# A hybrid decoder step on one core: the first projection from unnormed x, with the gates' and weights' first steps reordered

## The reference

```
h    = rmsnorm(x, norm1_w)              # x * rsqrt(mean(x^2) + 1e-6) * norm1_w, per token
proj = h @ w_in                         # columns: z, xBC, dt, u, q, k, v, and three gates
y_a  = SSD mixer(z, xBC, dt)            # causal conv, chunked scan, gated norm
y_b  = S5 mixer(u)                      # 32 groups of 16 channels, complex diagonal scan, GELU, GLU
y_c  = sliding-window attention(q, k, v)
mixed = sum over branches of sigmoid(gate) * (y @ w_branch)
x = x + mixed @ w_out
x = x + swiglu(rmsnorm(x, norm2_w)); y = rmsnorm(x, norm_f)
```

## Time and profile before

| | us |
|---|---|
| median of 3 runs | 1686.39 (1685.58 to 1688.41) |
| span of the profiled execution, first to last instruction | 1684.5 |
| TensorE busy | 1654.0 (98%) |
| VectorE, ScalarE, GpSimd busy | 966.9, 556.0, 791.2 |
| first product of u | 17.30 |
| first product of gate 0 | 69.16 |
| first product of gate 3 | 114.97 |

### The profile page before, as it was taken

The page is one execution under the profiler, slowest core; times in us unless marked ns, Lnnn a source line. Parts: engine busy times, 40 slices in busy tenths (PEclk is TensorE's granted clock), DMA queues, the critical chain, the costliest instruction groups (busy, mean ns, idle before and its releaser), DMA issues. The chain is left out here.

```text
span 1684.5 us, 30884 instructions
## 1 busy us (share of the span) xinstructions
PE 1654.0 (98%) x12241; PEld 1604.7 (95%) x12241; DVE 966.9 (57%) x1642; ACT 556.0 (33%) x1240; POOL 791.2 (47%) x756
## 2 busy tenths in 40 slices
PE   7999999999999999999999999999999999999997
PEld 7999999999999998888899999999999999999997
DVE  6859811406634554778873289666665565744346
ACT  5332121342213332543411154443443333322233
POOL 5483122322221111141322325877777777787774
PEclk9999999999999999999999999999999999999998
DMA  5364363232233234434365431543433344966443
GB/s 209 84 127 133 104 203 98 89 92 91 87 93 103 89 130 134 161 115 140 126 218 191 152 126 42 180 162 145 151 141 141 141 167 165 367 224 267 162 187 103
DMA packets 95805, 245.85 MB, mean 146 GB/s; under 512 B 14369, under 2 KB 42273, under 8 KB 95417
## 3 DMA queue, kind: packets, MB, share of 16 engines
q1 hardware_dynamic: 73824, 174.48, 30.5%
q0 software_dynamic: 10256, 33.59, 6.7%
q10 hardware_dynamic: 11592, 35.96, 6.3%
HBM read 177.11 MB, written 66.65 MB: 145 GB/s over the span
## 5 line engine op out<-in xcount | busy, mean ns | idle before, releaser
L1642 PE MATMUL ps<-HL,WH 128*128 128x384 f32 (+1 forms) x1536 | 507.7, 331 | 4.4 <-DVE HL L691 1.8
L1643 PE MATMUL ps<-HH,WL 128*128 128x384 f32 (+1 forms) x1536 | 497.4, 324 | 0.0
L1644 PE MATMUL ps<-HH,WH 128*128 128x384 f32 (+1 forms) x1536 | 496.3, 323 | 0.0
L1642 PEld LDWEIGHTS ps<-HL,WH 128*128 128x128 f32 x1536 | 289.4, 188 | 15.6 <-issue 9.3
L1643 PEld LDWEIGHTS ps<-HH,WL 128*128 128x128 f32 x1536 | 289.7, 189 | 0.3
L1644 PEld LDWEIGHTS ps<-HH,WH 128*128 128x128 f32 x1536 | 289.6, 189 | 0.0
L1285 POOL TENSOR_TENSOR WL<-WRAW,WH 128x1024 fp32r<-128x1024 f32 x59 | 145.0, 2457 | 243.3 <-DMA WH<-in_w 243.3
L1282 POOL DMA_DIRECT2D WH<-in_w x59 | 34.6, 586 | 354.4 <-PE ps L1644 352.9
L2932 DVE TENSOR_TENSOR X<-X,ps 128x528 f32<-128x528 f32 (+2 forms) x170 | 107.9, 656 | 155.5 <-PE ps L2238 104.6
L2327 ACT ACTIVATE GT<-ps 128x384 f32<-128x384 f32 (+1 forms) x72 | 33.4, 465 | 215.5 <-PE ps L1644 183.5
L2932 DVE TENSOR_TENSOR RB<-RB,ps 128x528 f32<-128x528 f32 x60 | 42.1, 701 | 103.4 <-ACT RB L2847 85.9
(11 more groups left out here) (467 smaller groups left out, 4266.2 us busy)
## 6 DMA issues: line engine op xcount, KB each, us to landing
WRAW<-in_w SPq DMA_DIRECT2D x75, 512.0 KB, 3.4
ffn_scratch<-STG SPq DMA_DIRECT2D x70, 528.0 KB, 3.6
WH<-in_w POOLq DMA_DIRECT2D x62, 512.0 KB, 4.6
SOP<-ffn_scratch SPq DMA_DIRECT2D x36, 528.0 KB, 7.9
gate_scratch<-GT ACTq DMA_DIRECT2D x24, 528.0 KB, 3.2
PX<-gate_scratch ACTq DMA_DIRECT2D x22, 528.0 KB, 4.2
HL<-ffn_scratch SPq DMA_DIRECT2D x22, 528.0 KB, 10.4
RAWB<-in_w SPq DMA_DIRECT2D x10, 1024.0 KB, 6.2
```

What stands on the lines that cost most here:

```text
L1642: nc.tensor.matmul(out, wh, rl, start=start, stop=False)
L1643: nc.tensor.matmul(out, wl, rh, start=False, stop=False)
L1644: return nc.tensor.matmul(out, wh, rh, start=False, stop=stop)
```

## The change

The first chunk of u is made from x times the norm weight, without the division by the root mean square. The products start as soon as x and the weights are split; the norm of that chunk is worked out later, and the tiles of u are multiplied by it on VectorE as they leave PSUM (`evict_first_u_dve`). The first chunk's h itself is split last (`SPLIT_ORDER` 1, 2, 0), as only the gates need it. The squares of a chunk are added in wider operations. Weights 0 and 1 are loaded as four halves from ScalarE's queue; SP's queue goes x, units 2 and 3, the second chunk of x, the bucket tables, the third chunk. The low parts of units 0 to 4 move from GpSimd to VectorE; GpSimd only counts them, and does the S5 constants earlier. TensorE starts with 92 products of a zeroed 128 x 128 tile. Of the gates, gate 0 takes its first chunk last, gate 1 follows at once, and taps and transposes of W come a gate later.

The core of the diff:

```diff
+    ROOT_ORDER = (1, 0, 2)
+    SPLIT_ORDER = (1, 2, 0)
+    FIRST_BY_ACT, SECOND_BY_ACT, SECOND_ADDS, THIRD_ADDS = 6, 6, 5, 5
...
+    def x_plain_high_act(k):
+        nc.scalar.wait_ge(s_x[k], 16)
...
+        nc.scalar.mul(HH[:, k, 0:384], X0[:, k, 0:384], prm("norm1", k, 1)).then_inc(xp_hi, 1)
+    def x_plain_low_dve(k):
+        dve.wait_ge(xp_hi, k + 1)
+        dve.scalar_tensor_tensor(HL[:, k, 0:384], X0[:, k, 0:384], prm("norm1", k, 1), HH[:, k, 0:384].bitcast(F32),
+                                 ALU.mult, ALU.subtract).then_inc(xp_lo, 1)
...
+    def x_second_sum_dve():
+        dve, pairs = nc.vector, GT[:, 0:768].rearrange("p (k c) -> p k c", c=384)
+        dve.wait_ge(s_xc[1], 128)
+        dve.tensor_tensor(pairs, X0[:, 6:8, 384:768], X0[:, 6:8, 384:768], ALU.mult).then_inc(pq_used, 1)
+        dve.wait_ge(pq_done, FIRST_BY_ACT + 4)
+        dve.tensor_tensor(SQ[:, 0:2], SQ[:, 0:2], SQ[:, 2:4], ALU.add).then_inc(pq_used, 1)
+        dve.wait_ge(pq_used, 2)
+        dve.tensor_tensor(SQ[:, 0:2], SQ[:, 0:2], pairs, ALU.add).then_inc(pq_used, 1)
+        dve.wait_ge(pq_done, FIRST_BY_ACT + SECOND_BY_ACT)
+        dve.wait_ge(pq_used, 3)
+        dve.tensor_tensor(SQ[:, 0:2], SQ[:, 0:2], HF0[:], ALU.add).then_inc(pq_used, 1)
+        dve.wait_ge(pq_used, 4)
+        dve.tensor_tensor(ACC[:, 384:768], SQ[:, 0], SQ[:, 1], ALU.add).then_inc(pq_used, 1)
...
+    def x_root_copy_act():
+        nc.scalar.wait_ge(pn_rs, 2)
+        nc.scalar.copy(GT[:, 0:384], x_spread_at(0)[:, 0:384]).then_inc(r0_ok, 1)
+    def evict_first_u_dve(j):
+        dve.wait_ge(r0_ok, 1)
+        dve.wait_ge(acc_done[0], j + 1)
+        dve.tensor_tensor(as_steps(UF[:, j, :], 0, 3), as_blocks(u_bank(j, 0), 3), as_blocks(GT[:, 0:384], 3),
+                          ALU.mult).then_inc(acc_free[0], 1)
...
         x_chunk(0)
+        first_weights(2)
+        first_weights(3)
+        x_chunk(1)
         sp.dma_start(HOT[:], io["hot"]).then_inc(s_hot, 16)
         sp.dma_start(RTAB[:], io["rtab"]).then_inc(s_hot, 16)
-        first_weights(0)
-        first_weights(1)
-        first_weights(2)
-        x_chunk(1, range(4))
-        x_chunk(1, range(4, KD))
-        first_weights(3)
...
+        nc.gpsimd.memset(IDB[:], 0.0).then_inc(consts_ok, 1)
...
+        def first_lows_counted():
+            pool.wait_ge(half_ok, 6)
+            pool.sem_inc(split_ok, 4)
+        def gate_low_counted():
+            pool.wait_ge(half_ok, 7)
+            pool.sem_inc(split_ok, 1)
...
         s5_angles()
-        split_halves()
-        u = 2
+        first_lows_counted()
+        s5_powers()
+        s5_rows()
+        s5_squarings(0)
+        gate_low_counted()
+        u = 5
...
+        pe.wait_ge(consts_ok, 2)
+        for _ in range(92):
+            nc.tensor.matmul(bank[4][:, 0:P], IDB[:], IDB[:], start=True, stop=True)
         pe.wait_ge(s_par, 16)
-        x_first_sums_pe()
-        bias_by_distance(0)
-        bias_by_distance(1)
-        x_spread_pe(0)
         u_pair(0, 0)
-        pe.wait_ge(bias_ev, 2)
-        u_pair(2, 0, {1: lambda: x_sums_pe(1), 3: lambda: x_spread_pe(1)})
-        u_pair(0, 1)
-        u_pair(2, 1, {1: lambda: x_sums_pe(2), 3: lambda: x_spread_pe(2)})
+        u_pair(2, 0, {1: lambda: bias_by_distance(0), 2: lambda: bias_by_distance(1), 3: lambda: x_sums_pe(1),
+                      5: lambda: x_spread_pe(1)})
+        u_pair(0, 1, {1: lambda: x_sums_pe(0), 5: lambda: x_spread_pe(0)})
+        u_pair(2, 1, {2: lambda: x_sums_pe(2), 4: lambda: x_spread_pe(2)})
         u_pair(0, 2)
         u_pair(2, 2)
...
-        gate(0, [0, 1])
+        gate(0, [1, 2])
+        gate(0, [0], lambda n, k: pe.wait_ge(h_lo, 2 * KD + k + 1))
+        gate(1, [0, 1])
         taps(0)
-        gate(0, [2])
         taps(1)
-        gate(1, [0])
+        gate(1, [2])
         taps(2)
-        gate(1, [1])
         taps(3)
-        gate(1, [2])
+        gate(2, [0])
         stt_rows(0)
-        for n in range(3):
-            gate(2, [n])
-            stt_rows(n + 1)
+        stt_rows(1)
+        gate(2, [1])
+        stt_rows(2)
+        gate(2, [2])
+        stt_rows(3)
...
+        for half in range(2):
+            c = slice(512 * half, 512 * half + 512)
+            for u in range(2):
+                act.dma_start(WRAW[:, u, c], io["w"][u][:, c]).then_inc(s_half0 if half == 0 else s_raw[u], 16)
...
+        for k in range(4, KD):
+            x_split_act(k, k + 1)
+            x_squares_act(2, [k])
+            if k == 6:
+                x_root_copy_act()
         evict_u(0, 1)
         evict_u(1, 1)
-        x_split_act(16, 24)
+        x_root_act(2)
+        x_split_act(8, 12)
         evict_u(2, 1)
+        x_split_act(12, 14)
         evict_u(3, 1)
+        x_split_act(14, 18)
+        evict_u(0, 2)
+        x_split_act(18, 19)
+        high_weights(4)
+        x_split_act(19, 20)
+        evict_u(1, 2)
+        x_split_act(20, 22)
+        high_weights(5)
+        x_split_act(22, 24)
...
+        x_plain_low_dve(0)
+        low_half_weights(0)
+        for k in range(1, 4):
+            x_plain_low_dve(k)
+        low_half_weights(1)
+        for k in range(4, KD):
+            x_plain_low_dve(k)
+        for u in (2, 3):
+            dve.wait_ge(first_high, u + 3)
+            tt(high_low(u)[1], WXR[:, u - 2, :], high_low(u)[0].bitcast(F32), ALU.subtract).then_inc(half_ok, 1)
         dve.wait_ge(den_ok, 1)
         nc.vector.reciprocal(SF("den"), SF("den")).then_inc(den_inv, 1)
+        x_first_rest_dve()
+        x_second_sum_dve()
+        x_first_add_dve(0)
+        x_recip_dve(1)
+        x_first_add_dve(1)
+        x_first_add_dve(2)
+        x_split_dve(0, 4)
+        x_recip_dve(0)
+        x_split_dve(4, 8)
+        x_third_sum_dve()
+        for j in range(3):
+            evict_first_u_dve(j)
         x_recip_dve(2)
+        evict_first_u_dve(3)
+        x_split_dve(8, 20)
+        dve.wait_ge(first_high, 7)
+        tt(high_low(4)[1], WRAW[:, 0, :], high_low(4)[0].bitcast(F32), ALU.subtract).then_inc(half_ok, 1)
+        x_split_dve(20, 24)
```

More of the change, by code:

```diff
@@ new lines, in x_first_squares_act, with x_first_rest_dve, x_first_add_dve @@
+    def x_first_squares_act(ks):
+        for k in ks:
+            nc.scalar.activation(SQ0[:, k, :], X0[:, k, 0:384], ACT.Square).then_inc(pq_done, 1)
+    def x_first_rest_dve():
+        dve, rest = nc.vector, slice(FIRST_BY_ACT, KD)
+        dve.tensor_tensor(SQ0[:, rest], X0[:, rest, 0:384], X0[:, rest, 0:384], ALU.mult).then_inc(x0_add, 1)
+    def x_first_add_dve(i):
+        dve = nc.vector
+        if i == 0:
+            dve.wait_ge(pq_done, FIRST_BY_ACT)
+        dve.wait_ge(x0_add, i + 1)
+        if i < 2:
+            n = 4 >> i
+            dve.tensor_tensor(SQ0[:, 0:n], SQ0[:, 0:n], SQ0[:, n:2 * n], ALU.add).then_inc(x0_add, 1)
@@ L786, in chunk_spread_pe @@
         last.then_inc(pn_rs, 1)
-    def pool_low(q, i):
-        return False
     def low_wait(eng, q, i):
[L794 to L797, removed]
+        eng.wait_ge(h_lo, HF_BASE[q] + i + 1)
     def norm_low_dve(q, i):
         m, dve, b = NORMS[q], nc.vector, HF_BASE[q]
-        if pool_low(q, i):
-            return
         n, k = divmod(i, KD)
@@ L1672, in unit, with gate @@
         def unit(u, slot, tiles):
[L1673 removed]
+            pe.wait_ge(*((half_ok, 7) if isinstance(u, int) and u == UNIT0["gates1"] else (split_ok, u + 1)))
             for args, kw in tiles:
                 tile(args[0], slot, *args[1:], **kw)
[L1677 removed]
+        def gate(g, chunks=range(3), before=None):
             u = (UNIT0["gates1"] + g) if g < 12 else (UNIT0["gates2"] + g - 12)
             no = (TILE0["gates1"] + g) if g < 12 else (TILE0["gates2"] + g - 12)
[L1680 removed]
+            unit(u, u % 2, [((no, 0, KD, HH, HL), dict(chunks=chunks, before=before))])
         def simple_loop(name, pairs, nk, RH, RL, skip=0, kbase=0, before=None):
@@ L1744, in bias_by_distance @@
                 pe.wait_ge(s_hot, 32)
-            nc.tensor.matmul(bank[2 + half][r:r + 8, 0:BHALF], RTAB[r:r + NBUCKET + 1, :], HOT[r:r + NBUCKET + 1, :], start=True,
+            nc.tensor.matmul(bank[5 + half][r:r + 8, 0:BHALF], RTAB[r:r + NBUCKET + 1, :], HOT[r:r + NBUCKET + 1, :], start=True,
                              stop=True).then_inc(bias_mm, 1)
@@ L2360, in bias_rows @@
             act.wait_ge(bias_mm, half + 1)
-            nc.scalar.copy(BT8[r:r + 8, :], bank[2 + half][r:r + 8, 0:BHALF]).then_inc(bias_ev, 1)
+            nc.scalar.copy(BT8[r:r + 8, :], bank[5 + half][r:r + 8, 0:BHALF]).then_inc(bias_ev, 1)
         def bias_spread(rnd, piece):
```

253 lines of the change are left out of this document (104 added, 149 removed).

## The result

The changed kernel takes 1691.03 us (median of 20 runs, 1687.3 to 1695.9) against 1685.93 for the kernel before (20 runs): ratio 1.0032, 95% interval 1.0026 to 1.0038. It is slower by 5.1 us where 4.5 us of gain were forecast; 1691.03 lies above the range.

A forecast was written before the change was run, and what follows sets the result against it. TensorE, busy 1654.0 of 1684.5 us, was taken as the bound. Gates beginning 5.9 us earlier and 1.4 of new waits gave -4.5: median 1681.9, own range 1679.5 to 1685, eight in ten 1677.5 to 1686.5.

The forecast's parts named there:

- When u can begin: Start of the kernel: first product of u at 9.2 us, once x and the first weights are loaded and split.
- The zeros: TensorE's start: 92 products of zeros at 0.08 us each take 7.4 us, end at 8.6, keep the clock up.
- case E: Opening of u: zeros don't raise the clock; slow steps cost 1.6 us inside the stall; chance within the forecast's 0.55.
- Rival D: Opening of u: zeros outlast the data and delay u; at 0.20 us each, 1690.6 us; chance 0.08.
- What is late next: In u: TensorE stalls 1.8 us for the second chunk's square sums; later stalls follow; gates begin at 63.3, 5.9 earlier.
- the stall at k = 7: In u's second chunk: 0.8 us lost, the high part queued on ScalarE behind the first chunk's spread copy.
- rival A: Loads at the start: data come sooner, stalls in u and half the gates' vanish; gain 8.1, 1678.3 us; chance 0.15.
- The gates: Between gate 0's and gate 3's first products: 45.8 us as before plus three waits, together 1.4 us.
- Rival C: In u: GpSimd's small operations slow VectorE's differences by 0.2 us a pair; gain 1.3, 1685.1 us; chance 0.08.
- The pairs of W transposes: In the gates: two pairs stand together, four banks' worth of copies through two; a wait of 0.5 us.
- rival B: In the gates: ScalarE held behind U's loads, W copies late; gain 1.5 to 2, 1684.6 us; chance 0.14.
- Behind it TensorE's order is as before: Behind gate 3's first product, at 114.97 us before: order unchanged, so the shift, -4.5 us, is passed on.

The follow-up runs named there:

- e3: The changed kernel without the 92 products of zeros at TensorE's start: 1687.78 us, ratio 1.0017 to the kernel before.
- e6: The kernel before with its four groups of taps put two and two on TensorE, nothing else changed: 1687.74 us, ratio 1.0011.
- e5: The changed kernel with GpSimd's subtraction of unit 5 held until VectorE's last split of x, and the taps taken apart: 1685.49 us, ratio 0.9996.
- e9: The changed kernel with only the taps taken apart, GpSimd's subtraction left in place: 1689.05 us, ratio 1.0015 to the kernel before.
- e10: e5 without the 92 products of zeros: 1684.18 us, ratio 0.9992 to the kernel before.
- e4: The kernel before with the 92 products of zeros put at TensorE's start, nothing else changed: 1688.71 us, ratio 1.0018.
- e12: e10 with GpSimd's subtraction of unit 6 held until W is made and gate 1 beginning with its second chunk: 1681.72 us, ratio 0.9981.

## Why the prediction was wrong

Step by step, in its order:

- *When u can begin*: right, 9.22 for 9.2. *The zeros*: right in size, 0.078 each for 0.08, end at 8.3 for 8.6; what case E says of a slow opening was right too (in e3, without the zeros, the opening is at the lower clock and the wait takes it up). Rival D, zeros that outlast the data, did not come.
- *What is late next*: the stall at k = 7 was 0.81 for 0.8, the one at the square sums 0.70 for 1.8, and the third chunk's sums waited 0.34, which I had not seen: 1.9 in all for 2.9. The square sums themselves came at 24.23 for 24.2, but TensorE was there at 23.5 and not at 22.4: 22 steps at the small groups, behind waits and at a new tile or k cost 0.05 to 0.16 beyond the usual one, 2.3 us together, where I had 0.3. The gates began at 64.8 and not at 63.3: gain 4.35 for 5.9. A term mis-sized, not the failure. The working has slips that change nothing here: 12.1, 5.6, 1.0 and -0.4 make 18.3 and not 18.7 (ScalarE's first square of that part of x began at 18.77, so rival A did not come either); the terms of its own range make 1680.2 to 1685.7; and the stretch from 20 to 25 of the kernel before moves 389 GB/s, more than the 378 called the most.
- *The gates* is the step that failed first: "The third chunk of gate 0 waits for ScalarE, which has the last evictions of u behind the first chunk's casts: 0.2." It measured 1.89, and with the step behind it 2.05; all in all the gates took 4.5 us more than before (50.3 for 45.8), where I had 1.4. I had seen the order of the queue, but priced the cast in front by its own time and not by what it waits for. I did not ask where GpSimd's unit 5 would now fall, though wide subtractions were in the earlier trace rows, with 4.36 beside them. That product takes x and the copied spread from SBUF (HF<-X,PRM,GT), where the other chunks' has the spread in PSUM. The kernel before shows a form with the spread in PSUM (and its result there too) beside a wide subtraction, and there it loses nothing (VectorE, then GpSimd):

```profile
20.91 0.62 DVE L702 SCALAR_TENSOR_TENSOR ps<-X,PRM,ps 128x384 f32<-128x384 f32 x1
```
```profile
19.51 4.93 POOL L1487 TENSOR_TENSOR WXL<-WXR,WXH 128x1024 fp32r<-128x1024 f32 x2 [2.31 <-ACT WXH L2344]
```

The Trainium skill, "SBUF — State Buffer", "Who interferes with whom", has a VectorE operation with two inputs in SBUF contend with a GpSimd operation that reads SBUF, and one with at most one such input, outside certain fast modes, not. 2.53 for the one form and 0.62 for the other agree. Rival C looked at the small operations and had the wrong ones.
- The pairs of W transposes: 1.55 and a hand-over for 0.5. This is rival B in part: U's loads started at 77.6, 1.1 later than before instead of 3.7 sooner (72.9), because of the same hold, and the gate store came late for ScalarE. Gate 1's wait of 0.67 was right (0.7). W was in time.
- "Behind it TensorE's order is as before, so a shift at that mark is passed on." This is the second failure and the larger: 0.15 at the mark became 5.1 in the median. A shift is passed on, but the clock is not the same thing in every run, and I had counted short products as work like any other. The rows that could have warned me were there: a fall at 386 with TensorE busy all the time, behind 18 products of 8 columns (383.6 to 385.6), in the timeline of before that I read:

```profile
383.56 1.95 PE L1916 MATMUL ps<-PRM,DTF 16*128 16x8 f32 x16
385.44 0.22 PE L1917 MATMUL ps<-PRM,DTF 16*32 16x8 f32 x2
```

What the runs put in its place: about 4 of the 5.1 us go with the clock; the paired short products are worth about 2 (e6, e5, e9), and the zeros, which I took for free, 1.3 to 3.2 (e10, e4, e3). These shares are read from different runs and do not add up to one sum.

Not settled: why the falls near 676 and 1052 are more frequent with the change than before, though at 1052 TensorE waits the same (2.12 us; at 676 it is 1.69 for 0.77), and by what way the zeros cost time. That they do is pointed to by e3, e4 and e10 (3.2, 2.9 and 1.3 us in the median) and by the count at 1045 to 1066; the intervals of e3 and e10 overlap with those of the kernels with zeros.

## What to carry to other kernels

When a step comes sooner, look up what it now runs beside: price an operation in a queue by what it waits for, and a VectorE operation with two inputs in SBUF by the wide GpSimd operation it may meet. Keep TensorE's waits and its short products apart, with long products between them; two groups of short products, 1.8 us each, put together cost 2 us here. Do not take it for granted that filling an idle start is free: 92 products of zeros at the start went with 1.3 to 3.2 us of loss. And read the spread of the runs and the mean granted clock with the median: one profile shows one draw.

## What the runs showed of the hardware

- The clock falls with TensorE busy throughout: behind 2.0 us of 8-column products (386), and behind 3.5 us of 32-column products (96 in e6). Behind idle times it fell after 1.7 us (676) and 2.1 us (1052), in some executions and not in others (the kernel before waits 2.1 us at 1049, and the clock stays up).
- Most falls last about 3.4 us and cost 1.4 to 1.6 us; one in e9 lasted 6.8. In e10 and e12 the profile had none from 14 to 1660.
- The granted clock of the opening may be recorded as 1.00 while products step at the lower level (kernel before) or truly (0.59, e4): the step between products is the surer sign.
- A 1024-wide subtraction on GpSimd (2.50) held a 384-wide VectorE product with both tensors in SBUF for 1.9 us, and a 2048-wide one for 2.2 (4.49 for 2.28, e5). The 384-wide form with one input tensor (and the result) in PSUM took 0.62 beside such a subtraction (kernel before, 20.91). Where the subtraction began after one of VectorE's operations, it was itself stretched (4.32, e5).
